# One set of y in the S5 mixer: eight transfers out and four in, time matrices in four column groups, bands made early

## The reference, cut to what matters

```python
def _modulate(x, c, g, w, b):
    m = (c @ w + b)[:, None, :]
    shift, scale, gate = jnp.split(m, 3, axis=-1)
    return _rmsnorm(x, g) * (1.0 + scale) + shift, 1.0 + gate

# _ab_mixer
proj = h @ w_in
ua, ub = proj[..., :512], proj[..., 512:]
ya = _pool_mixer(ua, ...)   # trailing means over 2, 4, 8, 16 tokens minus identity, then a linear map
yb = _s5_mixer(ub, ...)     # 32 groups of 16 channels, 64 complex states each
return concat([ya, yb]) @ w_out

# _s5_mixer: h_t = a h_(t-1) + B u_t ; y = Re(C h) + D u
y = gelu(y);  y = y * sigmoid(y @ w_glu + b_glu)
```

## Time and profile before

| | |
|---|---|
| median of 3 runs | 1289.25 us (1288.05 to 1290.51) |
| the profiled execution | 1290.38 us, span 1288.6 us |
| PE busy | 1241.1 us, 96% |
| DVE busy | 761.0 us, 59% |
| ACT busy | 448.7 us, 35% |
| POOL busy | 94.8 us, 7% |
| DMA | 157.40 MB, mean 122 GB/s |

### The profile page before, as it was taken

How to read it: one execution, slowest core, us unless ns; L and a number is a source line. 1 busy time by engine, 2 the same in 40 slices (tenths; PEclk the granted TensorE clock), 3 DMA queues, 4 the chain that set the end, 5 groups by cost and what they waited for, 6 DMA issues and landing times.

```text
span 1288.6 us, 16165 instructions
## 1 busy us (share of the span) xinstructions
PE 1241.1 (96%) x6192; PEld 1004.8 (78%) x6192; DVE 761.0 (59%) x1041; ACT 448.7 (35%) x611; POOL 94.8 (7%) x128
## 2 busy tenths in 40 slices
PE   6999599999999999999999998999999999999999
PEld 3788588788888888888779885567788888888887
DVE  7898777754654645655468957864643443443432
ACT  5442412421422312323443247862432231331321
POOL 0010012000000000051000001114100000000022
PEclk9999799999999999999999998999999999999999
DMA  9558755544445444431223220003143223223311
GB/s 322 187 116 261 244 192 197 172 160 154 146 168 171 171 163 131 171 112 58 83 70 122 82 89 1 1 1 98 33 131 98 76 98 92 92 98 98 98 65 65
DMA packets 132686, 157.40 MB, mean 122 GB/s; under 512 B 19784, under 2 KB 113152, under 8 KB 132608
## 3 DMA queue, kind: packets, MB, share of 16 engines
q1 hardware_dynamic: 125328, 153.82, 36.4%
q10 hardware_dynamic: 7312, 2.96, 1.1%
HBM read 151.39 MB, written 4.19 MB: 121 GB/s over the span
## 4 chain that ended last, share of the span: by engine, by line
PE 84%; DVE 9%; DMA 3%; ACT 2%; issue 1%; SPq 1%; ACTq 0%; POOL 0%; DVEq 0%
PE psum L1646 83%; PE psum L1650 2%; DVE ada_acc_b L1111 1%; DVE work L1294 1%; DMA ada_first<-in_ada_w 1%; DVE w_lo L1283 1%; DVE h_lo L1304 1%; DVE ada_acc L1111 1%; DMA raw_bn<-in_ssm_b_im 1%; DMA y_scratch<-y_run 1%; ACT pT L1034 1%; SPq L534 0%; DVE s_t L1082 0%; DVE rstd L1111 0%; DVE s_im L1082 0%
## 5 line engine op out<-in xcount | busy, mean ns | idle before, releaser
L1646 PE MATMUL psum<-h_hi,w_hi 128*128 128x512 f32 (+1 forms) x872 | 343.1, 393 | 3.4 <-DVE w_lo L1283 3.3
L1646 PE MATMUL psum<-h_lo,w_hi 128*128 128x512 f32 (+1 forms) x872 | 340.5, 390 | 0.0
L1646 PE MATMUL psum<-h_hi,w_lo 128*128 128x512 f32 (+1 forms) x872 | 340.4, 390 | 0.0
L751 ACT ACTIVATE w_hi<-w_raw 128x2048 fp32r<-128x2048 f32 x92 | 174.3, 1895 | 285.6 <-PE psum L1646 285.0
L1283 DVE TENSOR_TENSOR w_lo<-w_raw,w_hi 128x2048 fp32r<-128x2048 f32 x92 | 213.4, 2320 | 100.2 <-ACT w_hi L751 99.7
L1646 PE MATMUL psum<-a_hi,w_hi 128*128 128x512 f32 x512 | 202.4, 395 | 0.0
L1646 PE MATMUL psum<-a_hi,w_lo 128*128 128x512 f32 x512 | 202.2, 395 | 0.0
L1646 PE MATMUL psum<-a_lo,w_hi 128*128 128x512 f32 x512 | 202.1, 395 | 0.0
L1646 PEld LDWEIGHTS psum<-h_hi,w_hi 128*128 128x128 f32 (+1 forms) x872 | 164.0, 188 | 42.6 <-issue 7.2
L1646 PEld LDWEIGHTS psum<-h_hi,w_lo 128*128 128x128 f32 (+1 forms) x872 | 163.9, 188 | 35.0
L1646 PEld LDWEIGHTS psum<-h_lo,w_hi 128*128 128x128 f32 (+1 forms) x872 | 163.9, 188 | 33.8
(11 more groups left out here) (300 smaller groups left out, 1331.4 us busy)
## 6 DMA issues: line engine op xcount, KB each, us to landing
w_raw<-in_mlp_w SPq DMA_DIRECT2D x64, 1024.0 KB, 5.3
ada_l_ring<-in_ada_w SPq DMA_DIRECT2D x64, 384.0 KB, 6.1
w_raw<-in_cd_w_in SPq DMA_DIRECT2D x14, 1024.0 KB, 5.2
ada_more<-in_ada_w SPq DMA_DIRECT2D x20, 384.0 KB, 4.0
ada_first<-in_ada_w SPq DMA_DIRECT2D x5, 1024.0 KB, 15.4
ada_ring<-in_ada_w SPq DMA_DIRECT2D x12, 384.0 KB, 5.0
w_raw<-in_ab_w_in SPq DMA_DIRECT2D x4, 1024.0 KB, 7.4
w_raw<-in_ab_w_out SPq DMA_DIRECT2D x4, 1024.0 KB, 7.1
```

Of the source, the lines that this page charges most:

```text
L751: act.activation(w_hi[n % 2][:, :, 0:w], raw[n % 2][:, :, 0:w], ACT.Copy).then_inc(hi_ready, 1)
L1646: return nc.tensor.matmul(o, lhsT, rhs, start=start, stop=stop, **kw)
```

## The change

1. The 32 kr products and four skip products go to bank 0 alone, product t to the 32 partitions of column group t mod 4, with the group in the innermost loop. ACT copies two groups, DVE the other two in the middle of its first chain.
2. PE makes both Toeplitz halves, then all states. The second bank pair is released as before.
3. y leaves in one set of eight transfers of double size and returns in four. Behind it on SP's queue stand the loads that stood ahead of it (three row blocks and the slot `AB_OUT + 1`).
4. The bands lie in `ada_acc` and are made early: band 0 in front of a wait for ACT's sines, bands 1 to 3 in front of `first_scales`. `make_band` has five instructions instead of seven. POOL's index tile no longer waits for h.
5. The conditioning steps are dealt out anew: 20 instead of 25 ahead of the output projection, and 13 + 15 instead of 12 + 11 within it. `ada_sums` of unit 3 no longer waits for `ada_collect(2)`.

```diff
...
-        return work[g // 2][:, g % 2 * (BAND + PAD):g % 2 * (BAND + PAD) + BAND]
+        return ada_acc[:, g * (BAND + PAD):g * (BAND + PAD) + BAND]
...
-        return work[g // 2][:, g % 2 * (BAND + PAD) + BAND:(g % 2 + 1) * (BAND + PAD)]
+        return ada_acc[:, g * (BAND + PAD) + BAND:(g + 1) * (BAND + PAD)]
-    steps_off = work[0][:, 2 * (BAND + PAD):2 * (BAND + PAD) + BAND]
-    band_tmp = work[1][:, 2 * (BAND + PAD):2 * (BAND + PAD) + BAND]
+    steps_off = work[3][:, 0:BAND]
+    band_tmp = work[3][:, BAND:2 * BAND]
...
-    def y_rows(half, i):
-        return y_dram.rearrange("(g c) t -> c g t", c=C)[
-            :, half * GT:(half + 1) * GT, i * NRUN:(i + 1) * NRUN]
+    def y_rows(i):
+        return y_dram.rearrange("(g c) t -> c g t", c=C)[:, :, i * NRUN:(i + 1) * NRUN]
+    def kr_part(q):
+        return bank[0][2 * C * q:2 * C * (q + 1), :]
...
-        sp.wait_ge(mats_out, 12)
+        sp.wait_ge(kr_ready, 4)
         sp.wait_ge(toep_zero, 1)
...
               .then_inc(ada_mid_in[j], 16)
-        load(AB_OUT + 1, slots[AB_OUT + 1])
+        sp.wait_ge(y_copied, 4)
+        for i in range(1, RUN, 2):
+            sp.dma_start(y_rows(i), y_run[i * C:(i + 1) * C, :, :]).then_inc(y_out_s[0], 16)
+        sp.wait_ge(y_out_s[0], 16 * RUN)
+        for ct in range(4):
+            sp.dma_start(y_t[:, ct, :], y_dram[ct * P:(ct + 1) * P, :]).then_inc(y_in[ct // 2], 16)
         more_ada(3)
-        for half in range(2):
-            sp.wait_ge(y_copied, 2 * half + 2)
-            for i in range(1, RUN, 2):
-                sp.dma_start(y_rows(half, i), y_run[i * C:(i + 1) * C, half * GT:(half + 1) * GT, :])\
-                  .then_inc(y_out_s[half], 16)
-            sp.wait_ge(y_out_s[half], 16 * RUN)
-            for ct in (2 * half, 2 * half + 1):
-                sp.dma_start(y_t[:, ct, :], y_dram[ct * P:(ct + 1) * P, :]).then_inc(y_in[half], 16)
-        more_ada(6)
+        load(AB_OUT + 1, slots[AB_OUT + 1])
+        more_ada(5)
         load(AB_OUT + 2, slots[AB_OUT + 2])
...
         load(AB_OUT + 3, slots[AB_OUT + 3])
-        more_ada(15)
+        more_ada(16)
         assert ada_next[0] == 2 * ADA_STEPS - ADA_EARLY
...
         pool.tensor_copy(run_no[:, :], rot_c[:, 0, :].bitcast(I32)).then_inc(consts, 1)
-        pool.wait_ge(h_ready, 8)
         own(pool.iota(band_tmp.bitcast(I32), pattern=[[1, BAND]], base=0, channel_multiplier=-1))
...
         prep(GLU)
-        for i in range(8, 12):
-            act.wait_ge(mats_ps, i + 1)
-            t = (i - 8) * 4
-            act.activation(kr[:, t:t + 4, :].rearrange("p t n -> p (t n)"), bank[i % 2][0:2 * C, :],
-                           ACT.Copy).then_inc(mats_out, 1)
-        act.wait_ge(mats_out, 12)
+        act.wait_ge(mats_ps, 9)
+        for q in range(2):
+            act.activation(kr[:, q::4, :], kr_part(q).rearrange("p (t n) -> p t n", n=P), ACT.Copy)\
+               .then_inc(kr_ready, 1)
+        act.wait_ge(kr_ready, 4)
         act.wait_ge(toep_zero, 1)
...
                    .then_inc(y_copied, 1)
-            act.wait_ge(y_copied, 2 * half + 2)
-            for i in range(0, RUN, 2):
-                act.dma_start(y_rows(half, i), y_run[i * C:(i + 1) * C, half * GT:(half + 1) * GT, :])\
-                   .then_inc(y_out_s[half], 16)
+        act.wait_ge(y_copied, 4)
+        for i in range(0, RUN, 2):
+            act.dma_start(y_rows(i), y_run[i * C:(i + 1) * C, :, :]).then_inc(y_out_s[0], 16)
         for b in range(NB):
...
         tt(v(PH), v(PH), v(K_), SB)
+        def make_band(g):
+            win = float(WINDOWS[g])
+            ts(band_tmp, steps_off, 0.0, 1.0 / win, ALU.is_ge, M)
+            stt(band(g), steps_off, win, band_tmp, ALU.is_lt, M)
+            stt(band_tmp[:, 0:PAD], recip[:, :], 1.0 / win, band(g)[:, 0:PAD], ALU.max, M)
+            own(dve.scalar_tensor_tensor(out=first_band(g), in0=band_tmp[:, 0:PAD], scalar=win,
+                                         in1=ident[:, 0:PAD], op0=M, op1=SB))
+            tt(band(g)[:, 0:P], band(g)[:, 0:P], ident[:, :], SB)
+        dve.wait_ge(steps_ready, 1)
+        make_band(0)
         dve.wait_ge(setup_act, 5)
...
         dve.tensor_tensor(f_im[:, :, :, :], f_im[:, :, :, :], f_tmp_b[:, :, :, :], A).then_inc(f_ready, 1)
+        for g in range(1, 4):
+            make_band(g)
+        dve.sem_inc(bands, 1)
         first_scales()
...
             dve.sem_inc(inj_read, 1)
+            if half == 0:
+                dve.wait_ge(mats_ps, 9)
+                for q in range(2, 4):
+                    dve.tensor_copy(kr[:, q::4, :], kr_part(q).rearrange("p (t n) -> p t n", n=P))\
+                       .then_inc(kr_ready, 1)
             tt(flat(s_re), flat(s_re), flat(s_t1), A)
...
             chain(half)
-        def make_band(g):
-            win = float(WINDOWS[g])
-            for t, w in ((band(g), BAND), (first_band(g), PAD)):
-                tmp = band_tmp[:, 0:w]
-                if w == BAND:
-                    ts(tmp, steps_off, 0.0, 1.0 / win, ALU.is_ge, M)
-                else:
-                    ts(tmp, recip[:, :], 1.0 / win, None, ALU.max)
-                    stt(tmp, steps_off[:, 0:w], 0.0, tmp, ALU.is_ge, M)
-                stt(t, steps_off[:, 0:w], win, tmp, ALU.is_lt, M)
-                same = min(w, P)
-                tt(t[:, 0:same], t[:, 0:same], ident[:, 0:same], SB)
         def gelu_low(ct):
...
         ada_steps(8)
-        dve.wait_ge(steps_ready, 1)
-        for g in range(4):
-            make_band(g)
-        dve.sem_inc(bands, 1)
         prep(AB_OUT)
-        gelu_low(0)
-        gelu_low(1)
-        ada_steps(8)
-        gelu_low(2)
-        gelu_low(3)
-        ada_steps(2)
+        ada_steps(4)
+        for ct in range(4):
+            gelu_low(ct)
+        ada_steps(4)
         for g in range(4):
...
                                      in1=h_hi[:, g, :].bitcast(F32), op0=M, op1=SB).then_inc(cat_ready, 1)
-        ada_steps(7)
+        ada_steps(4)
         for m in range(4):
...
             prep(n + 1)
-            ada_steps((4, 4, 4, 0)[i])
+            ada_steps((6, 4, 4, 3)[i])
             for r in range(2):
...
-            pe.wait_ge(mods_part, unit if q is not None else unit - (unit > 3))
+            pe.wait_ge(mods_part, unit if q is not None else max(2, unit - 1))
             pe.wait_ge(ada_used, value - ADA_EARLY)
...
         pe.wait_ge(act_drain, drains[first_tile[AB_IN + 3] - 1][1])
-        for i in range(8, 12):
-            if i >= 10:
-                pe.wait_ge(mats_out, i - 1)
-            for r in range(4):
-                t = (i - 8) * 4 + r
-                o = bank[i % 2][0:2 * C, r * P:(r + 1) * P]
-                for n_, (b_, g_) in enumerate(((bd[0], g_re), (bd[1], g_ni))):
-                    mm(o, b_[:, t, :], g_[:, t, 0:RUN, :].rearrange("p m c -> p (m c)"), n_ == 0 and r == 0, False,
+        for t4 in range(GT // 4):
+            for b_, g_ in ((bd[0], g_re), (bd[1], g_ni)):
+                for q in range(4):
+                    t = 4 * t4 + q
+                    mm(kr_part(q)[:, t4 * P:(t4 + 1) * P], b_[:, t, :],
+                       g_[:, t, 0:RUN, :].rearrange("p m c -> p (m c)"), t4 == 0 and g_ is g_re, False,
                        skip_group_check=True)
-            t = (i - 8) * 4
-            mm(bank[i % 2][0:2 * C, :].rearrange("p (t n) -> p t n", n=P)[:, :, 0:C], ident[0:2 * C, 0:2 * C],
-               skip_d[:, t:t + 4, :], False, True, skip_group_check=True).then_inc(mats_ps, 1)
+        for q in range(4):
+            last = mm(kr_part(q).rearrange("p (t n) -> p t n", n=P)[:, :, 0:C],
+                      ident[0:2 * C, 0:2 * C], skip_d[:, q::4, :], False, True, skip_group_check=True)
+        last.then_inc(mats_ps, 1)
         slot_ready(AB_IN + 3)
...
-        def half_outputs(half):
-            toep_outputs(half)
+        toep_outputs(0)
+        pe.wait_ge(act_drain, drains[first_tile[GLU] - 1][1])
+        toep_outputs(1)
+        for half in range(2):
             pe.wait_ge(states, half + 1)
...
                 state_outputs(t)
-        half_outputs(0)
-        pe.wait_ge(act_drain, drains[first_tile[GLU] - 1][1])
-        half_outputs(1)
         pe.wait_ge(inj_read, 2)
```

More of the change, by code:

```diff
@@ L578, in _ @@
               .then_inc(ada_mid_in[j], 16)
-        load(AB_OUT + 1, slots[AB_OUT + 1])
-        more_ada(3)
-        for half in range(2):
-            sp.wait_ge(y_copied, 2 * half + 2)
-            for i in range(1, RUN, 2):
-                sp.dma_start(y_rows(half, i), y_run[i * C:(i + 1) * C, half * GT:(half + 1) * GT, :])\
-                  .then_inc(y_out_s[half], 16)
-            sp.wait_ge(y_out_s[half], 16 * RUN)
-            for ct in (2 * half, 2 * half + 1):
-                sp.dma_start(y_t[:, ct, :], y_dram[ct * P:(ct + 1) * P, :]).then_inc(y_in[half], 16)
-        more_ada(6)
+        sp.wait_ge(y_copied, 4)
[4 more added lines that the diff above has]
```

(4 more changed lines are left out.)

## The result

The changed kernel took 1307.95 us (median of 4, 1306.76 to 1308.99), the kernel before 1289.7 beside it (4 runs): ratio 1.0143, 95% interval 1.0125 to 1.016. Forecast were 1287.3, range 1281.0 to 1291.2. It is 18.3 us slower, where a small gain or nothing was expected. The profiled execution took 1308.6, its span 1306.9.

What follows compares the result with a forecast made beforehand. Bound: the path Toeplitz matrices, y, exchange, yg_lo, VectorE's list, 48 conditioning steps. Terms: -7.3 to the last h_lo, +1.1 tail, +4.2 clock, sum -2.0 from 1289.25, giving 1287.3 us; range 1281.0 to 1291.2.

Steps and rivals of the forecast that it cites:

- Bands: Early bands 1 to 3 ahead of VectorE's scale: 3.85 us, PE's second columns at 43, everything behind 1.9 us late.
- kr: PE's time matrices in four column groups: 2.4 us with skip products, done at 90.1 instead of 94.1.
- the rival in which column groups do not overlap: Third rival, chance 0.07: kr stays serial and ends at 96.1, y ends 5.3 us late, 1292.6 us.
- should take 58 alone: Injection record on PE: half kr's moving columns, so 58 ns alone against 29 measured, taken as overlap of two column groups.
- Exchange: y's transfers in one set: 7.6 us out to 127.6, back at 132.5, copies and last yg_lo done at 134.4.
- VectorE's list to the last h_lo: VectorE's work after y's return: 16.8 us plus 0.4 of starts, ending at 151.6 instead of 158.95.
- y takes 106.2 to 121.1 = 14.9 in any order: PE's y products keep their 14.9 us in the new order, starting at 103.9 and ending at 118.8.
- the tail: Last h_lo to last residual: 56.9 us against 55.75, +1.1, VectorE setting the pace, before the clock term.
- The clock term: Half clock on PE behind new waits of 5.2, 2 and 2 us in the output projection: +4.2 us, bounds 0 and 7.2.
- if such a load took more than that, every microsecond over would lengthen the tail: Loads costed at nothing, including the first MLP slot's, waiting for step 40 at about 186, read at about 193.
- The clock doesn't fall: First rival, chance 0.25: PE's clock stays up behind the projection waits, the 4.2 us is gone, 1283.1 us.
- slow exchange: Second rival, chance 0.13: y's exchange takes 11.3 us instead of 7.6, +3.7, 1291.0 us.

Runs made afterwards that it cites:

- a_fill: Changed kernel with four wide f32 products, result unread, ahead of PE's wait for the Toeplitz matrices: 1294.88 us, ratio 1.0005.
- c_tail2: a_fill with 14, 24, 14 and 28 wide products ahead of the four column sums in the output projection: 1289.54 us, ratio 0.9991.
- d_tail: a_fill with 11 VectorE steps instead of 4 ahead of yg_lo and seven wide products ahead of the last column sum: 1272.11 us, ratio 0.9842.
- b_kr: Kernel before with only kr made in four column groups, and four wide products ahead of the Toeplitz wait: 1280.32 us, ratio 0.9899.
- a_halves: Changed kernel with y's products in the old order, half by half, exchange still in one set: 1308.69 us, ratio 1.0104.
- d_nofill: Changed kernel, no fillers, with 11 VectorE steps instead of 4 ahead of yg_lo, 23 done at the last h_lo: 1286.01 us, ratio 0.9958.

## Why the prediction was wrong, point by point

**Right.** Bands: columns at 42.65 (43 forecast), all behind them 1.8 late (1.9). kr: 64 records in 1.9 us, 30 ns each against 116; the rival in which column groups do not overlap is refuted. The way there was weaker than it looked: "should take 58 alone" takes a record's time to go with its moving columns, but y's records, with 64 of them, took 118 ns each in the trace of before (3.79 us for 32), so 1.9 was right and the reason for it is not shown.

The rival had been read out of the Trainium skill, TensorE: Matmul & The Clock Gate, Part 3. Its sentence is about weight loads ("only when row_grp differs"), and a table of the same section gives three column tiles a measured speedup of 2.38, so the page as a whole does not say that kr stays serial. Here the trace goes against the sentence too: kr's weight loads, all on the same 128 rows, run beside its products and as closely, eight in 0.24 us.

Matrices: queued 92.22 (92.05), PE starts at 104.14 (103.9). Exchange: y out at 133.06, the transfers back issued at 139.66, so 6.6 us out (7.6), but 7.1 back (4.9): y is all back at 146.77, 13.7 after the copies (12.5). VectorE's list to the last h_lo: 17.1 (17.2). In a_fill, where nothing else is changed, y ends at 118.53 (118.8) and the last h_lo at 152.24 (151.6). Up to there the forecast was near but for the clock.

**Wrong, the step that decides: "y takes 106.2 to 121.1 = 14.9 in any order".** It took 27.7. The forecast itself had PE's tiles end at 101.3 and the matrices land at 103.9, a wait of 2.6 us, longer than the 2.25 us after which the earlier trace rows show the clock at half. It looked for clock costs only at the three waits of the tail, and priced each as a fall of some 5 us, as behind the waits of the earlier trace rows. What it did not ask is what stands behind the wait. In the old trace one fall ended within the band products (40 records of 16 to 144 moving columns, merged in the earlier trace rows under the last form) and the other within projection tiles of 512; y has 28 us at half clock of products with 64 and 63 columns that never ended it. 13.1 us by a_fill. No rival covered this.

**Wrong, the tail.** Forecast 56.9 plus 4.2 for the clock; measured 68.15. The clock term was near (5.0 by c_tail2, bounds 0 to 7.2), though there are four waits of 3.1 to 3.9 us and not three of 5.2, 2 and 2. The list was mis-sized: 62.8 at full clock, 5.9 over. Of this about 1 is the way to the second sum, 1.0 the first cycle (15.7 for 14.7) and 4.0 the second (18.65); about 1 of the 5.9 is the fillers' own (0.4 at the second sum, 0.65 at the fourth) and would fall to the clock. The forecast named the load of the MLP slot as a condition ("if such a load took more than that, every microsecond over would lengthen the tail") and gave it 7 us; it took 9, and steps of 3.4 took 4.3, one of them being a slow one beside a GpSimd sum, which the trace of before had already shown.

**Sum.** 13.1 for y and 5.9 + 0.8 for the tail are 19.8, the forecast's -2.0 added 17.8; measured 18.3 against 1289.7.

**The rivals.** "The clock doesn't fall" was the opposite of what happened; slow exchange and no overlap did not occur. The slower side of the forecast was looked for in a mechanism that was unlikely, not in the one that the forecast's own 2.6 us wait announced.

What stays open: which property of y's products left the clock down, what GpSimd's sums of squares do to the steps beside them, and how much one exchange instead of two gains by itself (between y's start and the last h_lo d_tail needs 45.1 us and b_kr 50.1, but bands and steps differ too).

## What to carry to other kernels

A wait on PE costs its length and can cost the clock after it, and how long the clock stays down depends on the work behind the wait. Before making a producer earlier or a consumer's cover shorter, look at what PE does next. In these runs the clock came back within products of 128 to 512 moving columns, and y's, of 63 and 64, ran at half speed to their end, 13 us for a 3.2 us wait; a few idle wide products into a free bank removed it. A wait near the edge is a risk and not a fixed price: the clock fell after waits of 1.16 and 1.36 us in one execution each and not after one of 1.34; after the 2.25 us wait ahead of the band products it fell in the kernel before and in a_halves, and not in the changed kernel and d_nofill. And where one engine's waits are free time, move the work there that will pace it later: seven of VectorE's steps moved into its wait for y were worth 20 us with all that followed (1294.9 to 1274.8).

## What the runs showed of the hardware that was not expected

The granted clock stayed at 1.2 GHz for 28 us (104.1 to 131.8 in the changed kernel) under unbroken f32 products of 64 moving columns and then 63 over 64 rows, and the same products ran at 2.4 GHz for 15 us in a_fill, where no wait stood in front of them. It came back within products of 128 columns (2.4 to 5.4 us after pool_w_t began, in five kernels) and within six products of 512 columns (they begin at 113.38, the clock is full from about 117.2). After a wait of 1.16 us in front of y's products it fell in one execution, 1.8 us after the wait had ended, where after one of 0.87 us it did not in another; behind 1.36 us ahead of column sums it fell, behind 1.34 it did not. In four column groups of 32 output partitions, 64 records of kr, all on the same 128 rows, took 1.9 us, 30 ns each, against 116 ns one after the other. A multiply-add of VectorE over 128x768 took 1.99 to 2.11 us instead of 1.02 each time that a GpSimd sum of 128x512 ran beside it (five of 25 in c_tail2), cause not isolated.
